# A hybrid decoder step on one core: keys and values laid out for the output by VectorE blocks and 128-byte stores instead of TensorE transposes

## What is computed

```python
def _mix_in(h, w_in):
    proj = h @ w_in
    q, k, v, b, c, hv = jnp.split(proj, [...], axis=-1)
    return q, k, v, b, c * hv          # q, k, v by head: 8 heads x 64

qp, kp, vp, bp, up = _mix_in(_rmsnorm(hp, norm_mix), w_in)     # prompt
qs, ks, vs, bs, us = _mix_in(_rmsnorm(hs, norm_mix), w_in)     # samples
attn_p = _combine([_branch_prompt(qp, kp, vp, d) for d in (1, 4, 16)])
attn_s = ...                           # samples against cache_k, cache_v
conv   = short_conv(...)
h = h + concat(rmsnorm(attn), rmsnorm(b * conv)) @ w_out
y = h + moe(rmsnorm(h))                # 32 experts, top 2 in the top group
return y_prompt, y_sample, k_prompt=kp, v_prompt=vp, ...       # kp, vp: (1024, 512)
```

## Time and profile before

| | |
|---|---|
| runs | 1094.33 us median (1093.88, 1094.33, 1096.39) |
| profiled execution, first to last instruction | 1093.2 us |
| outside it, median run less span | 1.1 us |
| PE busy | 1060.0 us, 97% of the span |
| DVE, ACT, POOL busy | 439.5, 281.0, 130.7 us |
| granted TensorE clock, mean | 0.993 |
| projection from 60 us to 319 us: PE busy | 258.1 of 259.0 us |
| prompt stores `k_prompt`, `v_prompt` | 2048 KB each, 9.6 and 14.2 us to landing |

### The profile page before, as it was taken

The page is one execution under the profiler, slowest core; times in us unless marked ns, Lnnn a source line. Parts: engine busy times, 40 slices in busy tenths (PEclk is TensorE's granted clock), DMA queues, the critical chain, the costliest instruction groups (busy, mean ns, idle before and its releaser), DMA issues.

```text
span 1093.2 us, 19671 instructions
## 1 busy us (share of the span) xinstructions
PE 1060.0 (97%) x8116; PEld 693.8 (63%) x8116; DVE 439.5 (40%) x1092; ACT 281.0 (26%) x610; POOL 130.7 (12%) x167
## 2 busy tenths in 40 slices
PE   8999999999999999999999999999999999997987
PEld 6899999999976766888754433444434444443323
DVE  5414433343158756888864421212211111111156
ACT  7212223211127863223121111111111111111114
POOL 1002210002100000000011121121111112021110
PEclk9999999999999999999999999999999999999999
DMA  7215482624133006112989999999999999999987
GB/s 257 75 40 169 133 280 65 230 58 136 59 107 108 3 28 245 67 78 105 408 352 403 401 421 420 419 419 421 419 419 420 419 418 420 419 417 420 420 321 289
DMA packets 78894, 292.65 MB, mean 268 GB/s; under 512 B 10610, under 2 KB 35338, under 8 KB 53906
## 3 DMA queue, kind: packets, MB, share of 16 engines
q1 hardware_dynamic: 62674, 247.09, 56.9%
q0 software_dynamic: 14960, 40.03, 10.3%
q10 hardware_dynamic: 1168, 4.23, 1.0%
HBM read 274.29 MB, written 32.07 MB: 280 GB/s over the span
## 4 chain that ended last, share of the span: by engine, by line
PE 79%; DMA 11%; SPq 5%; DVE 3%; ACT 1%; issue 1%; DVEq 0%; ACTq 0%
PE psum L1302 14%; PE psum L928 9%; PE psum L930 8%; DMA expert_w<-in_w_up 8%; PE psum L929 8%; PE psum L1360 6%; PE psum L1316 5%; SPq L787 5%; PE psum L1062 3%; PE psum L1064 3%; PE psum L1063 3%; PE psum L1343 2%; DMA y_tile<-y_rows 2%; PE psum L1013 2%; PE psum L1286 2%; PE psum L1029 1%
## 5 line engine op out<-in xcount | busy, mean ns | idle before, releaser
L1302 PE MATMUL psum<-expert_w,xT 128*64 128x512 f32 x512 | 228.4, 599 | 10.1 <-DMA expert_w<-in_w_up 9.9
L1304 PE MATMUL psum<-expert_w,xT 128*64 128x512 f32 x512 | 228.6, 599 | 0.0
L928 PE MATMUL psum<-h_hi,w_hi 128*128 128x344 f32 (+2 forms) x576 | 185.8, 323 | 3.1 <-DVE h_lo L1825 3.0
L930 PE MATMUL psum<-h_hi,w_lo 128*128 128x344 f32 (+2 forms) x576 | 184.0, 319 | 0.0
L929 PE MATMUL psum<-h_lo,w_hi 128*128 128x344 f32 (+2 forms) x576 | 183.9, 319 | 0.0
L1302 PEld LDWEIGHTS psum<-expert_w,xT 128*64 128x64 f32 x512 | 68.9, 138 | 145.9 <-issue 143.6
L1360 PE MATMUL psum<-expert_w,hT 128*64 128x512 f32 x512 | 116.9, 598 | 0.9 <-DVE hT L2421 0.9
L928 PEld LDWEIGHTS psum<-h_hi,w_hi 128*128 128x128 f32 x576 | 108.2, 188 | 5.6 <-DVE h_lo L1825 3.9
L930 PEld LDWEIGHTS psum<-h_hi,w_lo 128*128 128x128 f32 x576 | 108.3, 188 | 0.0
L929 PEld LDWEIGHTS psum<-h_lo,w_hi 128*128 128x128 f32 x576 | 108.2, 188 | 0.0
L2409 DVE TENSOR_TENSOR hid<-psum,silu_gate 64x512 f32<-64x512 f32 x32 | 21.9, 683 | 199.2 <-ACT silu_gate L1664 188.9
(11 more groups left out here) (337 smaller groups left out, 1400.0 us busy)
## 6 DMA issues: line engine op xcount, KB each, us to landing
expert_w<-in_w_gate SPq DMA_DIRECT2D x64, 1024.0 KB, 25.8
expert_w<-in_w_up SPq DMA_DIRECT2D x64, 1024.0 KB, 27.9
expert_w<-in_w_down SPq DMA_DIRECT2D x64, 1024.0 KB, 27.4
w_raw<-in_w_in SPq DMA_DIRECT2D x24, 512.0 KB, 4.0
y_tile<-y_rows SPq DMA_DIRECT2D x16, 512.0 KB, 13.9
kv<-in_cache_k POOLq DMA_DIRECT2D x24, 256.0 KB, 4.1
kv<-in_cache_v POOLq DMA_DIRECT2D x24, 256.0 KB, 4.7
x_tile<-in_x_prompt SPq DMA_DIRECT2D x8, 512.0 KB, 5.6
```

Of the source, the lines that this page charges most:

```text
L928: mm(ps, wh[:, k, :], h_hi[:, k, cols], start=(k == 0), stop=False)
L930: ins = mm(ps, wl[:, k, :], h_hi[:, k, cols], start=False, stop=(k == KD - 1))
L1302: mm(bank(0)[0:HEAD, :], xT[:, k, 0:HEAD], up[:, k, :], start=(k == 0), stop=(k == KD - 1), skip_group_check=True)
L1304: ins = mm(bank(0)[HEAD:P, :], xT[:, k, 0:HEAD], gate[:, k, :], start=(k == 0), stop=(k == KD - 1), skip_group_check=True)
```

## The change

Prompt keys and values are no longer turned on PE. After the last group of each k and v tile DVE turns the tile within 32x32 blocks, 128 partitions by 1024 tokens in one instruction, into `k_turned` (which takes the place of `kn`) or `v_turned` (the place of `v`), as soon as ACT has emptied all three groups. In such a block a partition holds 32 columns of one token, so a store to `k_prompt` moves runs of 32 numbers, 128 bytes. ACT's queue issues the stores, four for each tile (32 partitions each, 32 tokens by 32 blocks by 32 columns): those of k_i behind tile v_i, those of v_m behind tiles 12 to 15 (c0, u0, b0, c1). At tile c3 SP waits for all v stores and reads `v` back from `v_prompt`, into the place of `v_turned`; PE waits for that before its first use of `v`. Only the 8 sample rows of v are still turned on PE. Some semaphores are merged.

```diff
-        kn = at("kn", CT, [NQ, DA])
+        k_turned = at("k_turned", CT, [MA, SEQ])
+        v_turned = at("v_turned", XRES + 4 * MA * NTOK, [MA, SEQ])
...
                 if n == 0 and kind == "v" and m >= 1:
-                    groups += [("vn", m - 1, j) for j in range(3)]
+                    groups += [("vn", m - 1, 2)]
...
             if (kind, m) == ("v", MA - 1):
-                groups += [("kn", i, 0) for i in range(NQ)] + [("vn", MA - 1, j) for j in range(3)]
+                groups += [("vn", MA - 1, 2)]
...
-                    sp.dma_start(a["k_prompt"].rearrange("(t p) c -> p t c", p=P), kn).then_inc(kn_out, 16)
-                    sp.dma_start(a["v_prompt"].rearrange("(t p) c -> p t c", p=P), v).then_inc(v_out, 16)
                     sp.dma_start(a["k_sample"], srow[:, 1, :]).then_inc(out_misc, 16)
                     sp.dma_start(a["v_sample"], srow[:, 2, :]).then_inc(out_misc, 16)
+                if tiles[t] == ("c", 3):
+                    sp.wait_ge(v_out, 16 * MA * 4)
+                    sp.dma_start(v, a["v_prompt"].rearrange("(t p) c -> p t c", p=P)).then_inc(v_in, 16)
...
-                    for c in range(3):
-                        wait_emptied(pe, number["v", i, c])
-                    for c in range(4 if n < 2 else 1):
-                        t = 4 * n + c
-                        w = rows(t)
-                        ins = nc.tensor.transpose(ps[0:w, c * P:(c + 1) * P], vT[i % 2][:, t * P:t * P + w], ident)
-                elif kind == "kn":
-                    for m in range(MA):
-                        ins = nc.tensor.transpose(ps[:, m * P:(m + 1) * P], kT[:, m, i * P:(i + 1) * P], ident)
+                    wait_emptied(pe, number["v", i, 2])
+                    ins = nc.tensor.transpose(ps[0:NS, 0:P], vT[i % 2][:, SEQ:NTOK], ident)
...
+                if n == 0:
+                    pe.wait_ge(v_in, 16)
...
+            def store_turned(turned, name, m, count, out):
+
+                act.wait_ge(blocks_turned, count)
+                for b in range(P // 32):
+                    cols = slice(m * P + 32 * b, m * P + 32 * (b + 1))
+                    nc.scalar.dma_start(a[name][:, cols].rearrange("(j i) c -> i j c", i=32),
+                                        turned[32 * b:32 * (b + 1), m, :].rearrange("i (j c) -> i j c", c=32)
+                                        ).then_inc(out, 16)
...
                             act.wait_ge(group_done, number["vn", MA - 1, 2] + 1)
+                            act.wait_ge(blocks_turned, 2 * MA)
...
                             act.wait_ge(group_done, number["vn", i - 2, 2] + 1)
+                            act.wait_ge(blocks_turned, MA + i - 1)
...
+                if kind == "v":
+                    store_turned(k_turned, "k_prompt", i, i + 1, kn_out)
+                m = tiles.index((kind, i)) - 3 * MA
+                if 0 <= m < MA:
+                    store_turned(v_turned, "v_prompt", m, MA + m + 1, v_out)
...
                         if i == 0 and n == 0:
-                            dve.wait_ge(kn_out, 16)
+                            dve.wait_ge(kn_out, 16 * MA * 4)
...
+                if kind in "kv":
+                    for third in range(3):
+                        wait_emptied(dve, number[kind, i, third])
+                    source, turned = (kT[:, i, 0:SEQ], k_turned) if kind == "k" else (vT[i % 2][:, 0:SEQ], v_turned)
+                    vec.transpose(turned[:, i, :], source).then_inc(blocks_turned, 1)
```

More of the change, by code:

```diff
@@ L376, in program @@
         sval_clear = sem("sval_clear")
-        sval_copied = sem("sval_copied")
-        svalT_ready = sem("svalT_ready")
         scored = sem("scored")
@@ L382, in program @@
         u_ready = sem("u_ready")
-        sT_ready = sem("sT_ready")
+        blocks_turned = sem("blocks_turned")
+        v_in = sem("v_in")
+        sample_turned = sem("sample_turned")
+        sample_copied = sem("sample_copied")
         softmax_step = sem("softmax_step")
-        sexp_ready = sem("sexp_ready")
-        spT_ready = sem("spT_ready")
-        spT_copied = sem("spT_copied")
         spv_used = sem("spv_used")
@@ L731, in _ @@
                     sp.wait_ge(scored, NS + 1)
-                    sp.wait_ge(sT_ready, 1)
+                    sp.wait_ge(sample_turned, 1)
                     sp.dma_start(amask, a["amask"]).then_inc(attention_in, 16)
@@ L736, in _ @@
                     for m in range(MA):
-                        for j in range(3):
-                            wait_emptied(sp, number["vn", m, j])
+                        wait_emptied(sp, number["vn", m, 2])
                     for i in range(2):
                         wait_emptied(sp, number["rows", i, 0])
-                    for i in range(NQ):
-                        wait_emptied(sp, number["kn", i, 0])
-                    sp.dma_start(a["k_prompt"].rearrange("(t p) c -> p t c", p=P), kn).then_inc(kn_out, 16)
-                    sp.dma_start(a["v_prompt"].rearrange("(t p) c -> p t c", p=P), v).then_inc(v_out, 16)
                     sp.dma_start(a["k_sample"], srow[:, 1, :]).then_inc(out_misc, 16)
                     sp.dma_start(a["v_sample"], srow[:, 2, :]).then_inc(out_misc, 16)
+                if tiles[t] == ("c", 3):
+                    sp.wait_ge(v_out, 16 * MA * 4)
+                    sp.dma_start(v, a["v_prompt"].rearrange("(t p) c -> p t c", p=P)).then_inc(v_in, 16)
             sp.wait_ge(u_ready, MA)
@@ L752, in _ @@
                 sp.wait_ge(emptied, last)
-            sp.wait_ge(v_out, 16)
+            sp.wait_ge(v_out, 16 * MA * 4)
             sp.wait_ge(attention_in, 16)
@@ L864, in _ @@
             sp.wait_ge(out_misc, 16 * 4)
-            sp.wait_ge(kn_out, 16)
+            sp.wait_ge(kn_out, 16 * MA * 4)
         @block.tensor
@@ L946, in sample_probs_turned @@
                 nc.tensor.transpose(ps[0:NS, 192:256], sprob[:, 3 * P:3 * P + NS], ident[0:64, 0:64]
-                                    ).then_inc(spT_ready, 1)
+                                    ).then_inc(sample_turned, 1)
             def sample_values(b):
@@ L957, in sample_values @@
                 if b == 0:
-                    pe.wait_ge(spT_copied, 1)
+                    pe.wait_ge(sample_copied, 2)
                     pe.wait_ge(sval_clear, 1)
@@ L973, in sample_values_turned @@
             def sample_values_turned():
-                pe.wait_ge(sval_copied, 1)
+                pe.wait_ge(sample_copied, 3)
                 for b in range(NS):
                     ins = nc.tensor.transpose(bank(6, 2)[:, b * P:(b + 1) * P], sval[:, b, :], ident)
-                ins.then_inc(svalT_ready, 1)
+                ins.then_inc(sample_turned, 1)
             for g, (kind, i, n) in enumerate(groups):
@@ L1455, in unload_group @@
             if kind == "vn":
-                cols = slice(i * P, (i + 1) * P)
-                if n == 2:
-                    return copy(srow[:, 2, cols], ps[0:NS, 0:P])
-                return copy(v[:, 4 * n:4 * n + 4, cols], ps[:, :].rearrange("p (t c) -> p t c", t=4))
-            if kind == "kn":
-                return copy(kn[:, i, :], ps[:, :])
+                return copy(srow[:, 2, i * P:(i + 1) * P], ps[0:NS, 0:P])
         @block.scalar
@@ L1525, in _ @@
                     continue
+                if kind == "v":
[3 more added lines that the diff above has]
+                    store_turned(v_turned, "v_prompt", m, MA + m + 1, v_out)
                 if tiles.index((kind, i)) == VALUES_AT + NS // 2 - 1:
                     act.wait_ge(spv_ready, 1)
-                    nc.scalar.copy(kv[:, 0, 0:NS * P], bank(4, 2)).then_inc(sval_copied, 1)
+                    nc.scalar.copy(kv[:, 0, 0:NS * P], bank(4, 2)).then_inc(sample_copied, 1)
                 if tiles.index((kind, i)) == TURN_AT + 2:
@@ L1842, in _ @@
                     else:
-                        if kind == "v" and i >= 2:
-                            dve.wait_ge(group_done, number["vn", i - 2, 2] + 1)
                         ins = unload_group(dve, vec.tensor_copy, g)
@@ L1862, in _ @@
                 if t == VALUES_AT + NS // 2:
-                    dve.wait_ge(svalT_ready, 1)
+                    dve.wait_ge(sample_turned, 3)
                     values = bank(6, 2).rearrange("p (b c) -> p b c", b=NS)
@@ L1870, in _ @@
                 if t == TURN_AT + 1:
-                    dve.wait_ge(sT_ready, 1)
+                    dve.wait_ge(sample_turned, 1)
                     step(vec.tensor_reduce(smx, bank(6)[0:64, 0:3 * P + NS], X, ALU.max))
@@ L1874, in _ @@
                 if t == TURN_AT + 3:
-                    dve.wait_ge(sexp_ready, 1)
+                    dve.wait_ge(sample_copied, 1)
                     step(vec.reciprocal(srl, sl))
```

8 lines of the change are left out of this document (4 added, 4 removed).

## The result

The changed kernel takes 1098.94 us against 1094.41 us before (medians of 20 runs each); the ratio is 1.0042, 95% interval 1.0032 to 1.0053. It is slower by 4.6 us, where 6.3 us less was forecast, and it lies above the range. The span is 1097.6 us, before 1093.2.

The account below looks back on a forecast made before the run. PE, busy 97% of the span, was taken as the bound, with DVE, ACT and transfers free while behind it. 1094.3 - 2.4 - 3.9 = 1088.0 us; range 1086.8 to 1097.

Parts of the forecast that it names:

- Then ACT is held 1 + 107 x 0.036 = 4.9 us: Each group of four store issues holds ACT 4.9 us (ends 1.5 and 10.2), leaving 3.8 us spare, cost 0.
- a gain of 3.9 us at this place: End of v3: one small transpose waits for ACT's copy until 165.35; c0 starts at about 165.5 instead of 169.4.
- Rival 1: End of v3: zeros hold ACT, PE waits; gain shrinks to 1.7 us (1092.6) or 0.6 us (1093.7); chance 0.30.
- 6.4 runs to a packet: Beside the zeros, ACT's queue passes 6.4 runs to each other packet, 3.6 a microsecond; c0 starts at 167.7.
- 1.3 as the worse case: Beside the zeros, only 1.3 runs pass to each other packet; gain 0.6 us, 1093.7 us.
- the rival's own sum: ACT's issues beside the zeros: 36 of 107 runs gone by 162.5, the rest at 36 ns by 165.0.
- The eight transposes less in v1 to v3: PE drops eight of nine transposes inside each of v1, v2 and v3: 0.80 us each, 2.4 us saved.
- Rival 3: DVE's chain becomes the bound if a block transpose exceeds 5.7 us; at 7 us, 1098 us; chance 0.03.
- Rival 2: Short stores over 44 ns a run back up ACT, PE waits each tile: 1106 us at 55 ns; chance 0.14.
- SP's wait, the read of `v` and DVE's wait at b0: SP's wait at c3, the 2 MB read back (5.5 us within over 20) and DVE's wait at b0: cost 0.
- the 6.3 us of the sum: PE's total saving: 2.4 us inside v1 to v3 plus 3.9 us at the end of v3.

Follow-up runs that it names:

- the run with 4 KB: Changed kernel with the same 4 MB of zeros in the same place, cut into runs of 4 KB instead of 32 KB: 1097.50 us, ratio 1.0046.

## Why the prediction was wrong

**Where it went wrong: one term at one place.** The step that failed is "Then ACT is held 1 + 107 x 0.036 = 4.9 us", taken for all eight groups of issues and priced at nothing; from it follows that PE waits at the end of v3 only until ACT's copy at 165.35. For k0 and k1 the groups took 3.52 and 3.86 us; for k2, beside the zeros, 18.31, and PE waited 9.36 us. The forecast took a gain of 3.9 us at this place; the trace shows a loss of 4.94, and 2.45 more behind it.

**The mechanism was named, and mis-sized.** Rival 1 is what happened, with its place, its signs (one group of issues over 8 us in v3, PE idle behind the copy of `vT`) and its cause. It was given 0.30, and a gain at either of its rates. Its terms against what was measured:

- The zeros were to be through by 160 to 163; they land near 168, and the last of their 32 KB packets starts just before 166. They meet the stores because the change makes `w_lo`, and with it SP's queue, later: issued at 147.3 as forecast (147.6). Their end moved back with them and by some more (15.0 us to landing at most, 12.6 before); the forecast left it where it was.
- The turns: the forecast stood on 6.4 runs to a packet, read from 339 loads of 512 bytes beside 53 packets of POOL, with 1.3 as the worse case. The runs show turns by single packets, which makes 2 runs to a 32 KB packet of zeros, between the two. The row of the zeros themselves had the 4-byte packets in it, among its 89 under 512 bytes; why the row with 339 to 53 differs was not tried. The Trainium skill (DMA: Bandwidth & Descriptors, Queues, rings and completion order) has an engine drain a whole packet, typically 9 to 17 descriptors, before it switches queues. The traces agree that the queues take turns, but a turn of ACT's queue is one 128-byte run, and the measurement decides.
- ACT was to be free at 165.0, or by the sum at 1.3 at 166.1; it came free at 169.74. An estimate by the rival's own sum: with the zeros' end near 167 in place of 162.5, 6.4 runs to a packet give 169.0, and the measured rate (43 runs in 2 us on 16 engines, 1.34 to an engine and microsecond) gives 170.1. So the zeros' end was the larger error, some 4 us, and the rate the smaller, some 1. That the sum meets 169.74 is in part luck: its rule for letting an issue in, a count of runs, did not hold in the run with 4 KB. The step from there to c0, 2.7 us forecast, took 2.6.
- The lower clock behind a wait of 9 us was in no case of the prediction: 2.45 us.

The terms -2.66, +4.94 and +2.45 make the 4.73 us of the balance. A case in which the zeros' hold of ACT makes the kernel slower was therefore missing, and the range ended at 1097.0.

**What held.** The eight transposes less in v1 to v3 were forecast at 2.4 us and gave 2.66. A block transpose was taken at 1.23 us; the row of line 1857 in the changed kernel:

```profile
L1857 DVE STREAM_TRANSPOSE k_turned<-kT x4: 1245/1245/1246, 82.9 to 117.4; 128x1024 f32<-128x1024 f32 x4
```

Rival 3 needed 5.7. Without the zeros, a group of ACT's issues holds it 2.6 to 4.7 us behind v0 to v3 and up to 5.4 behind c0 to c1 in the kernels with the zeros moved, where 4.9 was taken. Rival 2 falls with the 1260 runs in a microsecond above: 16 engines x 1.024 us / 1260 = 13 ns a packet, the low end that the 160-byte stores had given. SP's wait, the read of `v` and DVE's wait at b0 cost nothing: between 60 and 320 us PE waits only at the one place. And the 6.3 us of the sum are there once the zeros are out of the way: 0.63 us of wait, as forecast for that place, and 6.9 us less in all, interval 5.1 to 8.6.

## What to carry to other kernels

An issue of a DMA is an instruction of the engine that makes it, and held that engine from 0.3 to 14.4 us here: cost it under the worst neighbour that will be in flight then, and let an engine issue it for which nobody waits. When a change delays a queue, list what else is in that queue and what it will now run beside; here what ran beside one group of stores decided between 0.6 and 9.4 us of waiting. Work that covers a wait, such as the transposes that looked like pure cost, also kept the clock up (c0's first group 4.05 us with dummy matmuls in the gap, 6.52 without); price its removal with the wait that it covered and with the stretch at the lower clock behind a long one.

## What the runs showed of the hardware

- ACT's queue of 128-byte runs and SP's queue of zeros take turns by single packets: 43 runs to 43 packets of q1, 22 of them 32 KB and 21 of 4 bytes; 167 to 169 with zeros of 4 KB; 707 to 612, not quite even, with 512 bytes. The runs fall from 1260 in a microsecond to about 20 beside 32 KB packets. It is not shown for every pair of queues: SP's 512-byte loads and POOL's packets went 339 to 53.
- An engine can stand in one issue of 128 KB for 14.4 us (ACT), SP for 10.9 in one and 17.08 in four.
- A packet of the block layout's stores, 128 bytes, takes 13 ns of a DMA engine, with its neighbours in memory 64 KB apart; a 512-byte packet of zeros takes 27 (51.6% of 2 us on 16 engines over 612). The Trainium skill (DMA: Bandwidth & Descriptors, Specifications) has transfers below 512 bytes read, modify and write. No run here shows what that costs, since the 160-byte stores that also take 13 ns lie below 512 bytes too.
- After 9.4 us without work PE ran c0's first products at the lower clock, 0.29 us apart where they are 0.155 apart at 2.4 GHz; with dummy matmuls in the gap it did not.
